# Columns of the first conditioning chunks: two plain transpositions and a reduction on VectorE in place of four selection products

## The chip, the core and the metric

One core of a Trainium2 chip runs the kernel as one program. The metric is the device time of that program in microseconds (us). The times given are of whole runs; a profile is of one execution, and its span (first to last instruction) is a little shorter than the run's own time.

## The reference

The reference is one step of a hybrid encoder layer for 640 tokens: 512 of one new stream and 16 of each of eight running streams. With c the conditioning vectors of the nine streams, it computes

```
sc  = silu(c)
mod = sc @ w_ada + b_ada                      # 9 x 1024 values a stream, split into shift, scale, gate
hn  = rmsnorm(x, norm_g) * (1 + scale1) + shift1
x   = x + 0.5 * gate1 * swiglu(hn, w1, w2)    # first feed-forward block
...
```

and then a mixer (a gated MLP beside a state-space scan), a second feed-forward block and a final modulated norm. The change lies in the first two parts of `mod`, shift1 and scale1 (2 x 1024 columns of w_ada), which the first feed-forward block needs before its first product.

## The kernel before

Activations lie transposed: features on the 128 partitions, the 640 tokens along the free axis, eight tiles of 128 features. The feed-forward products take float32 operands that are split into a high and a low part in fp32r, three products for each (`hn_hi`, `hn_lo` and the weights' `slot` pairs).

The first norm. Each of the eight token tiles of features (order `FIRST_TILE`) passes through four engines. VectorE multiplies the 512 prompt tokens by the inverse root (L2137, `hnf`), POOL does it for the 128 sample tokens (L745). Then the modulation: ScalarE scales and shifts the prompt part (L1596, in place in `hnf`), POOL the sample part (L762, L763). ScalarE copies the tile to `hn_hi` (L1602), VectorE subtracts to get `hn_lo` (L2143), and TensorE multiplies it with the weights of the first pair of hidden tiles (L1035, 12 products a tile). Between the tiles' work ScalarE and VectorE also split weight blocks (`slot`, L1546 and L2121).

The conditioning chunks. The 2 x 1024 columns come as eight chunks s of 256 columns (`ADA_FIRST`, order `FIRST_CHUNK`: a shift chunk, then the scale chunk of the same two feature tiles). A chunk takes these steps:

- `first_rows`, `cond_rows` (L985): TensorE multiplies the conditioning with the chunk. The contraction of 1024 is cut into eight pieces of 128, and piece k goes to the 32 partitions of row group k mod 4, so `ch_rows` in PSUM bank pair pC holds four partial sums, in row groups of 32 partitions of which nine are used.
- L1609: ScalarE copies the 128 x 256 partial sums to `ada_row` and raises `ch_row`.
- `first_cols`, `chunk_cols` (L993): for each of the chunk's two feature tiles TensorE multiplies the 128 x 128 block of `ada_row`, as stationary operand, with the selection matrix `quadsum` (128 x 9), which adds the four row groups and turns rows to columns in one go. `ch_tr` is raised. Before it TensorE waits for `ch_row` of this chunk, and for `ch_sum` of the chunk two before.
- `first_scale(q)` on VectorE (L2229, L2235), for the chunks 2q and 2q + 1: add the bias `b_col` to both, into `modc`, then (1 + scale) * norm_g in place, which raises `mod_ready`. ScalarE's L1596 and POOL's L762 wait for `mod_ready`.

The order of TensorE's work is written out by hand in `plain_first`: before the products of tile j it does the rows of the chunks in `FIRST_ROWS[j]` and the columns of those in `FIRST_COLS[j]`.

```
FIRST_ROWS = {0: (0, 1), 1: (2, 3), 2: (4,), 3: (5,), 4: (6, 7)}
FIRST_COLS = {0: (0, 1), 1: (2, 3), 3: (4, 5), 4: (6, 7)}
```

`keep_clock` issues products with no use (L1011), three behind the rows of chunk 0 and six before the products of tile 0. VectorE's order is that of `norm_first`: four L2137, `first_scale(0)`, two weight blocks, `hn_lo` of tile 0, two blocks, `hn_lo` of tile 1, four L2137, and then for each further pair of tiles `first_scale` and two `hn_lo`. ScalarE's order puts the copies L1609 of chunks 6 and 7 around `hn_hi` of tile 5.

Later chunks of the conditioning (`duo_rows`, `duo_cols`, `duo_sum`; L966, L977, L2221, L2222) use plain transpositions: L977 turns a 128 x 128 block with `nc.tensor.transpose`, and VectorE adds the parts.

Of the kernel before, what the change touches and what calls it, by code (L numbers as in the profile page):

```python
# [8 lines left out]
ALU = mybir.AluOpType  # L9
AX = mybir.AxisListType  # L10

P = 128
# [6 lines left out]
BANK = 512  # L19
# [3 lines left out]
NSTR = 1 + DEC_BATCH  # L23
# [13 lines left out]
QUAD = 32  # L37
# [47 lines left out]
def trunk_program(nc, x_prompt, x_sample, state_ssm, state_conv, c_prompt, c_sample, w_ada, b_ada, norm_g,  # L85
# [11 lines left out]
    def sem(name):  # L97
# [13 lines left out]
    modc = sb("modc", [P, MODT, NSTR])  # L111
    gate = sb("gate", [P, 3, KD * GRP])
    par = sb("par", [P, N_PAR])
    ident = sb("ident", [P, P])
# [15 lines left out]
    b_col = sb("b_col", [P, MODT])  # L130
    c_f32 = sb("c_f32", [P, KD, QUAD])
    quadsum = sb("quadsum", [P, QUAD])
# [89 lines left out]
    pB = ps("pB", 2 * BANK)  # L222
# [24 lines left out]
    ch_mm, ch_row, ch_tr, ch_sum = (  # L247
        sem("ch_mm"), sem("ch_row"), sem("ch_tr"), sem("ch_sum"))
# [100 lines left out]
    ch_rows = [pC[:, i * BANK:i * BANK + ADA_COLS] for i in range(2)]  # L349
    q_rows = [pB[:, q * ADA_COLS:(q + 1) * ADA_COLS] for q in range(2)]  # L350
    q_cols = [pB[:, BANK + q * 2 * P:BANK + (q + 1) * 2 * P] for q in range(2)]
    ch_cols = [pB[:, i * BANK:i * BANK + 2 * NSTR] for i in range(2)]


    xdt, xds = sq[:, 0:HG * HDIM], xadd[:, 0:HG * HDIM]
# [472 lines left out]
    def _(pe):  # L828
        mm = nc.tensor.matmul
# [101 lines left out]
        for k in range(KD):  # L931
            last = mm(pB[:, k * NSTR:(k + 1) * NSTR], c_sil[0:NSTR, k * P:(k + 1) * P], ident[0:NSTR, 0:NSTR],
                      start=True, stop=True)
        last.then_inc(c_tr, 1)

        for c in range(TT):
            pe.wait_ge(x_in[c], 16)
            wait(pe, xt_done, c - 1)
            for f in range(KD):
                last = nc.tensor.transpose(acc[c % 2][:, f * P:(f + 1) * P], x_row[c][:, f * P:(f + 1) * P],  # L940
                                           ident[:, :])
# [5 lines left out]
           start=True, stop=True).then_inc(par_tr, 1)  # L947
# [41 lines left out]
        def chunk_cols(i, m, bank, row):  # L989

            pe.wait_ge(ch_row, i + (m + 1))
            for f in range(2):
                last = mm(ch_cols[bank][:, f * NSTR:(f + 1) * NSTR], row[:, f * P:(f + 1) * P], quadsum[:, 0:NSTR],  # L993
                          start=True, stop=True)
            last.then_inc(ch_tr, 1)

        def first_rows(s):
# [250 lines left out]
        for c in range(TT):  # L1248
            last = mm(pC[:, c * QUAD:(c + 1) * QUAD], sq[0:2 * QUAD, c * P:(c + 1) * P], quadsum[0:2 * QUAD, :],
                      start=True, stop=True)  # L1250
# [13 lines left out]
        for j in range(CT):  # L1264
            dst = (acc[(U_Z + 1) % 2][0:TAIL, j * P:(j + 1) * P] if j < 8 else pC[0:TAIL, (j - 8) * P:(j - 7) * P])
            last = mm(dst, tails[:, j, :], ident[:, :], start=True, stop=True)
# [4 lines left out]
        for s in range(TT * SSD_G):  # L1271
            c, g = divmod(s, SSD_G)
            tok = slice(c * P, (c + 1) * P)
            dst = pB[:, s * P:(s + 1) * P] if c < ST else pC[:, BANK + g * P:BANK + (g + 1) * P]
            last = mm(dst, bcf[:, g, tok], bcf[:, SSD_G + g, tok], start=True, stop=True)
# [11 lines left out]
        for j in range(HP):  # L1287
            last = mm(pC[:, 3 * nh + j * DEC_BATCH:3 * nh + (j + 1) * DEC_BATCH],
                      gd[:, :, :].rearrange("p a b -> p (a b)")[:, j * P:(j + 1) * P], stream_of[:, :],
                      start=True, stop=True)  # L1290
# [110 lines left out]
        for j in range(HP):  # L1401
            last = nc.tensor.transpose(pC[:, j * P:(j + 1) * P], hst[:, j * P:(j + 1) * P], ident[:, :])
# [622 lines left out]
    def _(dve):  # L2025
        V = nc.vector
        st = Steps(dve, dve_step)
# [196 lines left out]
        def first_scale(q):  # L2224

            for s in (2 * q, 2 * q + 1):
                dve.wait_ge(ch_tr, s + 1)
                m = 2 * FIRST_CHUNK[s]
                V.tensor_tensor(out=modc[:, m:m + 2, :], in0=ch_cols[s % 2].rearrange("p (f c) -> p f c", c=NSTR),  # L2229
                                in1=b_col[:, m:m + 2].unsqueeze(2).broadcast_to([P, 2, NSTR]), op=ALU.add  # L2230
                                ).then_inc(ch_sum, 1)
            dve.wait_ge(ch_sum, 2 * q + 2)
            g = par[:, R_NORM + m - KD:R_NORM + m - KD + 2].unsqueeze(2).broadcast_to([P, 2, NSTR])
            v = modc[:, m:m + 2, :]
            V.scalar_tensor_tensor(out=v, in0=v, scalar=1.0, in1=g, op0=ALU.add, op1=ALU.mult).then_inc(mod_ready, 1)  # L2235
            dve.wait_ge(mod_ready, q + 1)
# [360 lines left out]
        s = ST * SSD_G  # L2597
# [205 lines left out]
```

## Time and profile before

| | |
|---|---|
| runs | 1444.98 us median of 3 (1444.59 to 1446.67) |
| the profiled execution, its own time | 1445.09 us |
| its span | 1443.5 us |
| TensorE (PE) busy | 1423.8 us, 99% of the span |
| VectorE (DVE) busy | 1014.8 us, 70% |
| ScalarE (ACT) busy | 662.8 us, 46% |
| POOL busy | 69.3 us, 5% |
| mean granted TensorE clock | 0.999 |

Busy time says how long an engine had instructions in it, not what it was worth. Matmuls overlap, so a row of the timeline that says 1.25 us for eight of them gives the time from the first's start to the last's end. A float32 product is issued as two instructions and is counted twice in the trace; a transposition with `nc.tensor.transpose` is counted once. PEld is the load of the stationary operand that goes before each of them.

### The profile page before, as it was taken

How to read it: one execution, taken by the hardware profiler on the slowest of the kernel's cores; microseconds unless marked ns; L12 is line 12 of the kernel's file. 1: busy time of each engine (PE TensorE's matmuls, PEld its weight loads, DVE VectorE, ACT ScalarE, POOL GpSimd, SP SyncE). 2: the span in 40 equal slices, each digit the busy share in tenths (PEclk: the TensorE clock that was granted, in tenths of full speed). 3: DMA queues.
4: the chain of work that ended last, by engine and by line, in shares of the span. 5: the costliest groups of instructions: out<-in, count | busy, mean ns of one | idle time of the engine just before them, and what ended most of it. 6: DMA issues, size and time to landing. Idle time of an engine off the chain costs nothing.

```text
span 1443.5 us, 25683 instructions
## 1 busy us (share of the span) xinstructions
PE 1423.8 (99%) x10212; PEld 1373.4 (95%) x10212; DVE 1014.8 (70%) x1742; ACT 662.8 (46%) x1186; POOL 69.3 (5%) x121
## 2 busy tenths in 40 slices
PE   7999999999999999999999999999999999999998
PEld 6899999999999999999789999998999999999997
DVE  5667667676777776667886567557767686767776
ACT  5543525253435444576825453226425253444354
POOL 3000000000000130000100000004000000000001
PEclk9999999999999999999999999999999999999999
DMA  9762434445344612231362222444314223231221
GB/s 304 208 196 66 153 116 143 121 133 160 110 139 132 183 31 74 74 93 55 98 187 77 68 73 64 131 144 122 110 56 144 66 89 88 69 107 52 81 74 74
DMA packets 219532, 161.02 MB, mean 112 GB/s; under 512 B 6826, under 2 KB 204646, under 8 KB 219426
## 3 DMA queue, kind: packets, MB, share of 16 engines
q1 hardware_dynamic: 217026, 153.87, 35.8%
q0 software_dynamic: 1696, 5.56, 1.3%
q8 instruction: 74, 1.21, 0.3%
q14 instruction: 32, 0.26, 0.1%
q10 hardware_dynamic: 704, 0.12, 0.0%
HBM read 151.50 MB, written 8.03 MB: 111 GB/s over the span
## 4 chain that ended last, share of the span: by engine, by line
PE 95%; DVE 2%; DMA 1%; ACT 1%; issue 0%; SPq 0%; POOL 0%; DVEq 0%; ACTq 0%
PE acc L844 25%; PE acc L1175 19%; PE pC L1066 19%; PE acc L1066 14%; PE acc L1054 4%; PE acc L1124 2%; PE pB L966 2%; PE acc L1035 1%; DMA ada_raw<-in_w_ada 1%; PE pC L1315 1%; PE pB L925 1%; PE pB L1300 1%; PE pC L1450 1%; PE pC L1334 1%; PE acc L861 0%; DVE y_row L2761 0%
## 5 line engine op out<-in xcount | busy, mean ns | idle before, releaser
L1546 ACT ACTIVATE slot<-raw 128x512 fp32r<-128x512 f32 (+1 forms) x310 | 189.5, 616 | 237.8 <-PE acc L1175 137.7
L2121 DVE TENSOR_TENSOR slot<-raw,slot 128x512 fp32r<-128x512 f32 (+1 forms) x310 | 208.1, 675 | 53.1 <-ACT slot L1546 50.6
L1175 PE MATMUL acc<-hid_hi,slot 128*128 128x320 f32 x1240 | 238.4, 310 | 0.0
L1066 PE MATMUL pC<-hn_hi,slot 128*128 128x320 f32 x912 | 216.3, 309 | 0.0
L1175 PEld LDWEIGHTS acc<-hid_hi,slot 128*128 128x128 f32 x1240 | 195.1, 188 | 2.9 <-issue 2.1
L844 PE MATMUL acc<-hn_hi,whi 128*128 128x320 f32 x672 | 160.9, 321 | 0.0
L1066 PEld LDWEIGHTS pC<-hn_hi,slot 128*128 128x128 f32 x912 | 156.2, 188 | 2.5 <-issue 2.5
L844 PE MATMUL acc<-hn_hi,wlo 128*128 128x320 f32 x672 | 153.1, 309 | 0.0
L844 PE MATMUL acc<-hn_lo,whi 128*128 128x320 f32 x672 | 152.9, 309 | 0.0
L1066 PE MATMUL acc<-tT,slot 128*128 128x320 f32 x912 | 146.3, 309 | 0.0
L1175 PE MATMUL acc<-hid_lo,slot 128*128 128x320 f32 x620 | 142.0, 308 | 0.0
L1066 PE MATMUL pC<-hn_lo,slot 128*128 128x320 f32 x456 | 140.8, 309 | 0.0
L1066 PEld LDWEIGHTS acc<-tT,slot 128*128 128x128 f32 x912 | 136.5, 188 | 0.0
L844 PEld LDWEIGHTS acc<-hn_hi,whi 128*128 128x128 f32 x672 | 111.9, 188 | 6.3 <-issue 5.9
L844 PEld LDWEIGHTS acc<-hn_lo,whi 128*128 128x128 f32 x672 | 112.3, 188 | 0.0
L844 PEld LDWEIGHTS acc<-hn_hi,wlo 128*128 128x128 f32 x672 | 112.2, 188 | 0.0
L1175 PEld LDWEIGHTS acc<-hid_lo,slot 128*128 128x128 f32 x620 | 103.8, 188 | 0.0
L2065 DVE TENSOR_TENSOR xadd<-acc,gate 128x128 f32<-128x128 f32 x95 | 27.6, 290 | 91.4 <-PE acc L1175 77.5
L2035 DVE TENSOR_TENSOR wlo<-wraw,whi 128x1024 fp32r<-128x1024 f32 x50 | 61.0, 1222 | 38.2 <-ACT whi L1528 37.6
L1066 PEld LDWEIGHTS pC<-hn_lo,slot 128*128 128x128 f32 x456 | 85.6, 188 | 0.0
L2059 DVE SCALAR_TENSOR_TENSOR xT<-acc,gate,xT 128x320 f32<-128x320 f32 (+1 forms) x190 | 82.6, 475 | 0.2 <-PE acc L861 0.2
L1066 PE MATMUL pC<-tT,slot 128*128 128x320 f32 x456 | 73.2, 309 | 0.0
(389 smaller groups left out, 2414.9 us busy)
## 6 DMA issues: line engine op xcount, KB each, us to landing
raw<-in_ffn_w SPq DMA_DIRECT2D x88, 512.0 KB, 5.2
sraw<-in_w_ada SPq DMA_DIRECT2D x26, 1024.0 KB, 6.5
wraw<-in_w_in SPq DMA_DIRECT2D x36, 512.0 KB, 3.8
raw<-in_ffn_w SPq DMA_DIRECT2D x16, 1024.0 KB, 5.1
ada_raw<-in_w_ada SPq DMA_DIRECT2D x8, 1024.0 KB, 11.7
wraw<-in_w_out SPq DMA_DIRECT2D x16, 512.0 KB, 4.1
raw<-in_ffn_w SPq DMA_DIRECT2D x8, 768.0 KB, 4.4
sraw<-in_w_ada_final SPq DMA_DIRECT2D x6, 1024.0 KB, 7.5
```

What stands on the lines that cost most here:

```text
L844: last = mm(acc[p][:, h * BANK:h * BANK + HALF], w[:, k, :], a[:, k * TOK + h * HALF:k * TOK + (h + 1) * HALF], start=(k == 0 and t == 0), ...
L925: last = nc.tensor.transpose(out[:, c * P:(c + 1) * P], src[:, c * P:(c + 1) * P], ident[:, :])
L966: last = mm(q_rows[lane_of(duo)][q * QUAD:(q + 1) * QUAD, :], c_f32[:, k, :], kxn(duo_raw(duo, j), KD, ADA_COLS)[:, k, :], start=(kk == 0) ...
L1054: last = mm(half(acc[d], h), w[:, kk * P:(kk + 1) * P], a[:, k * TOK + h * HALF:k * TOK + (h + 1) * HALF], start=(k == 0 and t == 0), stop ...
L1066: last = mm(out, w[:, kk * P:(kk + 1) * P], a, start=(first and kk == 0 and t == 0), stop=(kk == KQ - 1 and t == 2), skip_group_check=not ...
L1124: last = mm(a[h], w[t // 2][:, k, :], (hid_hi, hid_lo)[t % 2][:, k * TOK + h * HALF:k * TOK + (h + 1) * HALF], start=(k == 0 and t == 0), ...
L1175: last = mm(a[h], w[t // 2][:, k, :], (hid_hi, hid_lo)[t % 2][:, k * TOK + h * HALF:k * TOK + (h + 1) * HALF], start=(k == 0 and t == 0), ...
L1546: A(slot_as(fi, b, 0), source_of(fi, b), ACT.Copy).then_inc(blk_hi, 1)
L2035: V.tensor_tensor(out=weights(n, i, 1, w), in0=wraw[p][:, 0:w], in1=weights(n, i, 0, w).bitcast(F32), op=ALU.subtract).then_inc(wlo_done, 1)
L2059: return V.scalar_tensor_tensor(out=x[:, s:e], in0=a[s // HALF][:, p:p + e - s], scalar=gate[:, q, f * GRP:f * GRP + 1], in1=x[:, s:e], op ...
L2065: V.tensor_tensor(out=by_stream(xadd[:, SEQ:TOK]), in0=by_stream(a[1][:, SEQ - HALF:HALF]), in1=g, op=ALU.mult)
L2121: V.tensor_tensor(out=slot_as(fi, b, 1), in0=source_of(fi, b), in1=slot_as(fi, b, 0).bitcast(F32), op=ALU.subtract).then_inc(blk_lo, 1)
```

## The change

For the first eight chunks the two selection products become two plain transpositions with the identity. A transposition only turns the block, so the four row groups come out as four groups of 32 columns, and `ch_cols` is 256 columns wide instead of 18. VectorE then adds the four groups with a `tensor_reduce` (nine columns used of each), and adds the bias in an instruction of its own, in place in `modc`. `ch_sum`, for which TensorE waits before it writes the bank again, now follows the reduction. VectorE waits for its own reduction before the bias, and for the bias before it goes on.

```diff
-    ch_cols = [pB[:, i * BANK:i * BANK + 2 * NSTR] for i in range(2)]
+    ch_cols = [pB[:, i * BANK:i * BANK + 2 * P] for i in range(2)]
...
             pe.wait_ge(ch_row, i + (m + 1))
             for f in range(2):
-                last = mm(ch_cols[bank][:, f * NSTR:(f + 1) * NSTR], row[:, f * P:(f + 1) * P], quadsum[:, 0:NSTR],
-                          start=True, stop=True)
+                last = nc.tensor.transpose(ch_cols[bank][:, f * P:(f + 1) * P], row[:, f * P:(f + 1) * P], ident[:, :])
             last.then_inc(ch_tr, 1)
...
             for s in (2 * q, 2 * q + 1):
                 dve.wait_ge(ch_tr, s + 1)
                 m = 2 * FIRST_CHUNK[s]
-                V.tensor_tensor(out=modc[:, m:m + 2, :], in0=ch_cols[s % 2].rearrange("p (f c) -> p f c", c=NSTR),
-                                in1=b_col[:, m:m + 2].unsqueeze(2).broadcast_to([P, 2, NSTR]), op=ALU.add
-                                ).then_inc(ch_sum, 1)
-            dve.wait_ge(ch_sum, 2 * q + 2)
+                part = ch_cols[s % 2].rearrange("p (f k c) -> p f c k", f=2, c=QUAD)[:, :, 0:NSTR, :]
+                V.tensor_reduce(out=modc[:, m:m + 2, :], in_=part, axis=AX.X, op=ALU.add).then_inc(ch_sum, 1)
+                dve.wait_ge(ch_sum, s + 1)
+                st.done(V.tensor_tensor(out=modc[:, m:m + 2, :], in0=modc[:, m:m + 2, :],
+                                        in1=b_col[:, m:m + 2].unsqueeze(2).broadcast_to([P, 2, NSTR]), op=ALU.add))
```

On TensorE, at the columns of chunks 0 and 1 (one row stands for the four instructions of a pair of chunks; each pair has the same):

```order
-L993 MATMUL pB<-quadsum,ada_row 128x9 x4
-L1011 MATMUL acc<-upto,ident 128x256 x6
-L1035 MATMUL acc<-hn_hi,slot 128x320 x2
...
+L993 MATMUL pB<-ident,ada_row 128x128 x4
+L1010 MATMUL acc<-upto,ident 128x256 x6
+L1034 MATMUL acc<-hn_hi,slot 128x320 x2
```

Nothing changes its place; four products with nine columns to stream become four transpositions with 128, and all line numbers behind fall by one.

On VectorE, at `first_scale(1)`, between the products with the inverse root and the low parts of tiles 2 and 3:

```order
-L2137 TENSOR_TENSOR hnf<-xT,rT 128x512 x4
-L2229 TENSOR_TENSOR modc<-pB,b_col 128x18 x2
...
+L2136 TENSOR_TENSOR hnf<-xT,rT 128x512 x4
+L2229 TENSOR_REDUCE modc<-pB 128x18
+L2231 TENSOR_TENSOR modc<-modc,b_col 128x18
+L2229 TENSOR_REDUCE modc<-pB 128x18
+L2231 TENSOR_TENSOR modc<-modc,b_col 128x18
 L2235 SCALAR_TENSOR_TENSOR modc<-modc,par 128x18
```

Two instructions ahead of the scale became four, each behind the one before it. The same is so in all four calls.

## Rows read from the trace of the kernel before

**Rows 1.** The profile's page, busy time of TensorE, share of the span, instructions
```profile
PE 1423.8 (99%) x10212; PEld 1373.4 (95%) x10212; DVE 1014.8 (70%) x1742; ACT 662.8 (46%) x1186; POOL 69.3 (5%) x121
```

**Rows 2.** Waits of TensorE, whole span: us in total, times, longest
```profile
PE acc L1035 <- DVE hn_lo L2143: 2.6, 3, 1.8
...
PE acc L1054 <- ACT tmp L1706: 0.4, 1, 0.4
```

**Rows 3.** Chain that ended last, from 20 us: start, us, what
```profile
22.85 0.41 DVE modc L2235
...
23.35 0.81 ACT hnf L1596
...
27.07 2.02 PE acc L1035 x12
...
32.38 0.19 DVE modc L2235
...
35.34 2.02 PE acc L1035 x12
...
44.72 0.19 DVE modc L2235
...
51.26 0.60 ACT tmp L1706
...
51.99 14.32 PE acc L1054 x96
```

**Rows 4.** Timeline, TensorE's column products and weight loads of chunks 6 and 7
```profile
43.19 1.28 PE L993 MATMUL pB<-quadsum,ada_row 128*128 128x9 f32 x8
...
43.86 0.52 PEld L993 LDWEIGHTS pB<-quadsum,ada_row 128*128 128x128 f32 x4 [0.15 <-issue]
```

**Rows 5.** Timeline, ScalarE's copies of chunks 3 and 7, and `hn_hi` between
```profile
31.02 0.38 ACT L1609 ACTIVATE ada_row<-pC 128x256 f32<-128x256 f32 x1 [0.48 <-PE pC L985]
...
43.37 0.38 ACT L1609 ACTIVATE ada_row<-pC 128x256 f32<-128x256 f32 x1
```

**Rows 6.** Timeline, the transpositions of a later chunk, loads and products
```profile
82.14 0.29 PEld L977 LDWEIGHTS pB<-ident,srow 128*128 128x128 f32 x2
82.29 0.38 PE L977 MATMUL pB<-ident,srow 128*128 128x128 f32 x2
```

**Rows 7.** Timeline of VectorE, `first_scale` of pairs 1 and 3
```profile
31.54 0.18 DVE L2229 TENSOR_TENSOR modc<-pB,b_col 128x18 f32<-128x18 f32 x1
32.17 0.18 DVE L2229 TENSOR_TENSOR modc<-pB,b_col 128x18 f32<-128x18 f32 x1 [0.46 <-PE pB L993]
32.38 0.18 DVE L2235 SCALAR_TENSOR_TENSOR modc<-modc,par 128x18 f32<-128x18 f32 x1
...
43.51 0.82 DVE L2143 TENSOR_TENSOR hn_lo<-hnf,hn_hi 128x640 fp32r<-128x640 f32 x1 [0.82 <-ACT hn_hi L1602]
44.25 0.44 DVE L2229 TENSOR_TENSOR modc<-pB,b_col 128x18 f32<-128x18 f32 x2
```

**Rows 8.** VectorE's reductions and small additions, ns min/median/max or mean
```profile
L2221 DVE TENSOR_TENSOR modc<-pB,b_col x18: 184/188/191, 83.2 to 1133.0; 128x36 f32<-128x36 f32 x18
...
L2202 DVE TENSOR_REDUCE quadsum<-ident x1: 371/371/371, 6.0 to 6.0; 128x32 f32<-128x128 f32 x1
...
L2664 DVE TENSOR_REDUCE stat<-pB 128x5 f32<-128x640 f32 x8 | 6.6, 827 | 2.0 <-PE pB L925 2.0
```

**Rows 9.** Timeline of POOL, its eight products for the sample tokens
```profile
17.72 5.51 POOL L745 TENSOR_TENSOR hnf<-xT,rT 128x128 f32<-128x128 f32 x8 [11.14 <-ACT rT L1556]
```

**Rows 10.** Stretches: length, busy time and instructions of each engine, granted clock (PEclk)
```profile
10.00:15.00 5.00, 4.65 (x30) 4.17 (x29) 4.35 (x4) 4.89 (x10) 0.00 (x0) 1.00 0.78 242
24.00:27.00 3.00, 1.29 (x6) 0.79 (x5) 2.21 (x4) 3.00 (x7) 1.05 (x3) 1.00 1.01 324
1436.00:1438.00 2.00, 0.35 (x4) 0.11 (x1) 2.00 (x4) 0.00 (x0) 0.00 (x0) 1.00 1.03 381
1438.00:1440.00 2.00, 0.00 (x0) 0.00 (x0) 2.00 (x4) 0.00 (x0) 0.00 (x0) 0.82 1.03 382
```

## The prediction

> **What bounds the kernel now.** Read the busy times first: TensorE had instructions in it for 99% of the span [rows 1]. Then its waits, because only where it waits can something else set the end: over the whole span it waits for `hn_lo` three times, 2.6 us in all, and once 0.4 us for ScalarE's `tmp` [rows 2]. Everything that the change touches lies between 18 and 50 us. So the question is when TensorE can begin the product row L1054, at 51.99 in the chain [rows 3]. From there the chain is almost nothing but TensorE until the last norm, so a shift of that moment should reach the end in full.
>
> What does 51.99 hang on? Follow the chain back. TensorE waits there for ScalarE's `tmp`, which starts at 51.26, and ScalarE is fed without a break by what `first_scale(3)` released: VectorE's last scale at 44.72 [rows 3]. Between the two lie the modulation of tiles 6 and 7, a table load, three weight blocks and the silu, all in ScalarE's own order: 51.99 - 44.72 = 7.27 us of fixed work. The first product of tile 0 (27.07) and that of tile 2 (35.34) hang in the same way on the scales at 22.85 and 32.38 [rows 3]. The eight chunks are thus a latency chain (rows on TensorE, copy on ScalarE, columns on TensorE, `first_scale` on VectorE), four times over, each beginning where the last one let TensorE or ScalarE go on. I price the change by how much later each of the four scales starts.
>
> **TensorE's side.** Before, a chunk's columns are four records, a pair of chunks eight; now a chunk has two. If TensorE were the bound this would count in full, but the second chunk of a pair has to wait for its copy. Chunk 7's copy runs 43.37 to 43.75 [rows 5], and its first weight load starts at 43.86 [rows 4], 0.11 later. Chunk 3's copy ends at 31.40 [rows 5] and VectorE is released by that chunk's columns at 32.17 [rows 7]. So the second chunk's columns begin when ScalarE is ready, before and after. What the first chunk's columns save turns into a wait for the copy, and I cost it at nothing; its cover is that copy, and were the copy earlier by 0.3 us, the saving would show. What counts is the second chunk's own length, from first load to result. Before, the products' row ends at 43.19 + 1.28 = 44.47, that is 0.61 us behind the load at 43.86 [rows 4]. A pair of transpositions runs from 82.14 to 82.29 + 0.38 = 82.67, so 0.53 us [rows 6]. That is a gain of 0.08; I take 0.1, as VectorE's start needs its few hundredths either way. The bounds are 0 and 0.2.
>
> **VectorE's side.** Before, an addition is followed by the scale 0.21 us later (32.17 to 32.38 [rows 7]). Now the same path is reduction, bias, scale. The bias reads 18 elements and should cost the 0.21 once more. The reduction reads 72 elements of PSUM and is not in the trace in this shape. Its bounds are 0.18 us (an addition of 18 elements [rows 7]) and 0.37 (the reduction of 128 elements, the engine's first instruction [rows 8]). Between them, an addition of 36 elements takes 0.188 and the reduction of 640 elements 0.827 [rows 8], a slope of 0.64 / 604 = 1.06 ns an element, which gives 0.188 + 36 x 1.06 ns = 0.23 us. I take 0.23, as 72 is much nearer to 36 than to 640, and 0.26 from its start to the next one's. So a chunk takes 0.26 + 0.21 = 0.47 us of VectorE, where it took 0.21.
>
> **The four pairs.** The delay of each scale against the one before it:
> - Pair 0. The columns give 0.1 back, the second chunk's path grows by 0.26: +0.16. POOL is still in its eight products until 17.72 + 5.51 = 23.23 [rows 9], and the scale at 22.85 took 0.41 where the later ones take 0.19 [rows 3]. The added bias instructions meet the same company, up to +0.22 each; or the scale itself, coming later, is rid of it, -0.22. I take +0.2, with ends of 0 and +0.5.
> - Pair 1. VectorE comes to it at 31.54 [rows 7], when the first chunk is ready; reduction and bias take it to 32.01, before the second chunk's 32.07. So +0.26 - 0.1 = +0.16.
> - Pair 2. VectorE waits there for both chunks. +0.16 again.
> - Pair 3. Here VectorE is late itself: `hn_lo` of tile 5 starts at 43.51 and the two additions come right behind it, at 44.25 and at 44.51, where the second was just released [rows 7]. Before, the scale began 44.72 - 44.25 = 0.47 us behind the first addition. Now two reductions and two biases stand there, 2 x 0.47 = 0.94 us. So +0.47, and the columns' gain is worth nothing, since chunk 7 is ready (44.4) before VectorE has done with chunk 6 (44.7).
>
> The sum is 0.2 + 0.16 + 0.16 + 0.47 = 0.99, so **+1.0 us**. On TensorE it first appears as a longer wait ahead of tile 0 (1.8 us, the longest one [rows 2]) and ahead of tile 2, then as a new wait of some 0.4 us ahead of tile 6, whose `hn_lo` hangs on pair 3; and then L1054 begins 1.0 us later. Nothing is moved in any queue, no DMA is added, and the loads wait for the chunks' rows, not for their columns. The span becomes 1443.5 + 1.0 and the profiled execution 1445.09 + 1.0 = 1446.1. That execution lies 0.1 above the median of the three runs, 1444.98, so the median becomes **1446.0 us**. About 0.2% (2.9 us) is what a measurement of this kernel can tell from no change; the runs themselves span 2.1 us. The forecast is well inside it.
>
> The Trainium skill speaks against this sum: "Perfetto Trace Analysis", section "Transposes", says to use a transpose and not a standard matmul for what is logically a transposition, since it skips the arithmetic. By it the sum would be a gain, that of the first rival. No sentence above rests on it.
>
> **The rivals.**
> - *TensorE paces it, and the columns' saving counts.* Before, the eight records of a pair occupy 1.28 us [rows 4]. Two transpositions occupy 0.38 [rows 6], so four take at most 0.76. That saves 0.52 a pair and 2.1 us over four: 1442.9 us, or, where it counts only in a pair or two, up to 1444.6. For it speaks that TensorE is busy 99% [rows 1]; against it the copy that ends only 0.11 ahead of the load [rows 4, 5]. Chance 0.12. Even whole it stays within 0.2%.
> - *The reduction is slow.* Groups of four elements, 32 apart, in PSUM may cost as the 0.37 row does [rows 8]. Then +0.14 in pairs 0 to 2 and +0.28 in pair 3, 0.7 more, and with pair 0 at its upper end 1.0 more: 1446.7 to 1447.0 us. Chance 0.15.
> - *The clock falls.* This one is slower than before for certain. Transpositions might not count as work, and TensorE is idle longest right behind them, 1.8 us ahead of tile 0 [rows 2]. With pair 0 that becomes 2.0. At the end of the program TensorE is idle from about 1436.4, and the granted clock is 1.00 until 1438 and 0.82 over the next two microseconds [rows 10], so it fell at 1438 + 2 x 0.64 = 1439.3, some 2.9 us into the idle time. From about that length on this rival decides; 2.0 is short of it, and the half-busy stretch 24 to 27 was at 1.00 [rows 10]. Were it to fall to its lower level of 1.2 GHz at 27.07, the work until the columns of pair 1 (27.07 to 31.5) would take twice as long, +4.4: with the forecast's 1.0, 1450.4 us. Chance 0.05.
> - *The shift is swallowed.* A later wait of TensorE with another cause than the shifted engines could take it in. Against it speaks that the chain goes on from 51.99 with TensorE without a break, 14.32 us in its first row alone [rows 3]. Time 1445.0. Chance 0.08.
>
> On the clock, row and rule part. TensorE did little but transpositions between 10 and 15 us, 30 instructions in 4.65 us, at a granted 1.00 [rows 10]; so the transpositions that are added do not lower it by themselves. The Trainium skill, "TensorE: Matmul & The Clock Gate", section "Part 4: PE-mode transpose", says that the full clock doesn't engage for transposes, as they don't count as busy in the same way. By the rule the time would be the clock rival's 1450.4, by the row the forecast's.
>
> **How the numbers follow.** Forecast 0.60, the four rivals 0.12, 0.15, 0.05 and 0.08. The forecast's own range is 1445.4 to 1446.6 by the bounds of pair 0 and of the columns. For 8 in 10 it has to reach to the slow reduction, 1447.0, and take in the swallowed shift and the smaller part of TensorE's saving, 1444.6; with a few tenths on either side for the median of a few runs, **1444.3 to 1447.3**. Faster by over 0.2% means below 1442.1, beyond even the whole of TensorE's saving: 0.02. Slower by over 0.2% means above 1447.9: the clock rival and a small rest, 0.06. Within: 0.92.
>
> **What the next profile shows.** The second chunk's transpositions start about 0.1 us behind ScalarE's copy, with TensorE waiting for it in each pair, and end 0.5 us later. Reductions of 0.23 us and bias additions of 0.18. The first, second and fourth scale start at about 23.0, 32.7 and 45.7; tile 0's products at 27.3, tile 2's at 35.7, L1054 at 53.0. The granted clock stays 1.00 until the last microseconds. I am wrong if L1054 starts no later than 51.99 (TensorE paced the stretch), if the reduction takes over 0.35, or if L1054 is late by 1.0 and the end is not.

## The result and the profile after

| | kernel before | changed kernel |
|---|---|---|
| median of 20 executions each | 1445.54 us | 1448.20 us |
| lowest, highest | 1444.59, 1449.39 | 1446.44, 1450.74 |
| ratio | | 1.0018, 95% interval 1.0012 to 1.0025 |
| profiled execution, own time and span | 1445.09, 1443.5 us | 1450.30, 1448.7 us |
| TensorE busy | 1423.8 us | 1425.0 us |
| VectorE busy | 1014.8 us | 1017.0 us |
| mean granted clock, this execution | 0.999 | 0.996 |

The changed kernel is slower by 2.7 us by the medians and 2.6 by the means, where 1.0 was forecast, and its time lies above the range of 1444.3 to 1447.3. The median of 1448.20 is 2.2 above the forecast's 1446.0, and 0.56 of that is the kernel before itself, whose median over 20 executions is 1445.54 and not the 1444.98 of the first three. Counted from that kernel the range ended at +2.3, and 2.7 is above that too. The ratio is below the 0.2% that was called no change, while its interval reaches beyond 0.2% and leaves out a ratio of 1.

Start where the prediction said the answer would stand, with the chain, which answers to [rows 3]. The rows give start, length and what ran.

```profile
23.01 0.19 DVE modc L2235
...
27.00 2.47 PE acc L1034 x12
29.47 3.06 PE pC L985 x32
...
34.08 0.19 DVE modc L2235
...
37.03 2.02 PE acc L1034 x12
...
41.65 0.19 DVE modc L2235
...
46.95 0.19 DVE modc L2235
...
54.22 5.81 PE acc L1053 x38
```

L1054 of before is L1053 now, and it starts at 54.22 instead of 51.99. Two rows give the first clue. Tile 0's products take 2.47 us from start to the next piece, those of tile 2 2.02 as before; and the rows of chunks 2 and 3 take 3.06 us, where the chain of before has 1.86 for the same 32 records:

```profile
29.09 1.86 PE pC L985 x32
```

Nothing in the change touches these. The stretches (length, then busy time and instructions of PE, PEld, DVE, ACT and POOL, then the granted clock, the DMA's share and GB/s) say why:

```profile
24.00:26.00 2.00, 0.74 (x4) 0.31 (x2) 1.28 (x2) 2.00 (x5) 0.98 (x3) 1.00 1.05 343
26.00:28.00 2.00, 1.00 (x7) 1.00 (x8) 2.00 (x4) 1.97 (x4) 0.00 (x0) 1.00 1.07 344
28.00:30.00 2.00, 2.00 (x15) 1.44 (x18) 1.83 (x4) 0.28 (x1) 0.00 (x0) 0.59 1.09 356
30.00:32.00 2.00, 2.00 (x28) 0.94 (x24) 1.55 (x3) 0.38 (x1) 0.00 (x0) 0.56 1.09 347
32.00:34.00 2.00, 1.76 (x21) 1.15 (x10) 0.78 (x4) 0.38 (x1) 0.00 (x0) 1.00 1.09 348
...
622.00:624.00 2.00, 2.00 (x9) 1.75 (x8) 1.68 (x3) 1.16 (x3) 0.00 (x0) 0.57 0.60 144
```

In the kernel before, the same stretches stand at 1.00:

```profile
28.00:30.00 2.00, 2.00 (x28) 1.46 (x30) 1.83 (x4) 0.35 (x1) 0.00 (x0) 1.00 1.10 351
30.00:32.00 2.00, 1.95 (x29) 1.30 (x21) 1.72 (x4) 0.77 (x2) 0.00 (x0) 1.00 1.09 348
```

In the changed kernel the granted clock fell to its lower level of 1.2 GHz at about 28.4 and came back shortly before 32. It did not fall while TensorE idled but 1.4 us after it had taken up tile 0. It fell a second time near 622 us. The timeline of TensorE shows what stood ahead of the first fall:

```profile
21.13 1.01 PE L993 MATMUL pB<-ident,ada_row 128*128 128x128 f32 x4
21.98 2.76 PE L1010 MATMUL acc<-upto,ident 128*128 128x256 f32 x12
27.00 0.56 PE L1034 MATMUL acc<-hn_hi,slot 128*128 128x320 f32 x2 [2.26 <-DVE hn_lo L2142]
```

In the kernel before the same three pieces were

```profile
21.42 1.19 PE L993 MATMUL pB<-quadsum,ada_row 128*128 128x9 f32 x8
22.46 2.84 PE L1011 MATMUL acc<-upto,ident 128*128 128x256 f32 x12
27.07 0.56 PE L1035 MATMUL acc<-hn_hi,slot 128*128 128x320 f32 x2 [1.77 <-DVE hn_lo L2143]
```

The wait ahead of tile 0 is 2.26 us; it was 1.77. Two things lengthen it: VectorE gives `hn_lo` later, and TensorE is through with the unused products earlier, because the transpositions ahead of them are short.

VectorE's new instructions, ns min/median/max, are as priced but for one bias addition of 0.455 us, and answer to [rows 8]:

```profile
L2229 DVE TENSOR_REDUCE modc<-pB x8: 225/232/233, 21.6 to 46.5; 128x18 f32<-128x72 f32 x8
...
L2231 DVE TENSOR_TENSOR modc<-modc,b_col x8: 177/178/455, 21.9 to 46.7; 128x18 f32<-128x18 f32 x8
```

The distances along the latency chain, in us, tell latency and clock apart. Each is the difference of two starts; "rows 1" is the start of the rows of chunk 1, scales are L2235, "products" is L1054 or L1053. The last columns belong to experiments below.

| from, to | before | change | predicted addition | e1, nine unused products | e4, one group |
|---|---|---|---|---|---|
| rows 1, tile 0 | 6.65 | 6.87 | 0.20 | 6.66 | 6.26 |
| tile 0, scale 1 | 5.31 | 7.08 | 0.16 | 5.52 | 5.28 |
| scale 1, scale 2 | 7.41 | 7.57 | 0.16 | 7.57 | 7.24 |
| scale 2, scale 3 | 4.93 | 5.30 | 0.47 | 5.31 | 4.88 |
| scale 3, products | 7.27 | 7.27 | 0 | 7.27 | 7.28 |
| sum | 31.57 | 34.09 | 0.99 | 32.33 | 30.94 |

From tile 0 to scale 1 the fall of the clock sits: with it 7.08, without it 5.47 to 5.52 (e1, e13, and e10, a second profile of the change). So the clock cost 1.6 us there, and the latency is 0.22 + 0.16 + 0.16 + 0.37 = 0.9 us in this execution. The 0.22 of pair 0 is its least certain part. The other three profiles of the change (e10, e14, e15) have 6.59, 6.59 and 6.60 us from rows 1 to tile 0, and the five profiles with the columns and VectorE's part of before have 6.43 to 6.65. The first scale starts 0.17 later (2.60 us behind rows 1 against 2.43), but in the profile of before it took 0.40 us itself, and in these three 0.18. The whole distance from rows 1 to products is 32.20 to 32.33 us in e1, e10 and e13, which have no fall near 28, and 31.57 before: 0.6 to 0.8 us of latency. The profiled execution started this stretch 0.29 earlier, hence 2.23 at L1053 and not 2.52. From there to the end 3.0 us more are lost, none of them in the change's reach: 0.9 by 107 us, where a load of `raw` came late and TensorE waited 0.7 us behind it, 1.5 in the fall near 622, and 0.6 around a load of `gm_bias`, for which TensorE waited 0.7. These differ from one execution to the next, as the experiments show, so one pair of profiles can't be subtracted.

### The profile page after: what moved, and what is told of

It reads as the page before. It is cut to its first block, busy times and chain, and to the rows that moved or that the text cites. A ratio compares the mean times of both kernels' runs of the same rounds, so it can differ in the third digit from the quotient of the medians.

```text
span 1448.7 us, 25663 instructions
## 1 busy us (share of the span) xinstructions
PE 1425.0 (98%) x10196; PEld 1372.4 (95%) x10196; DVE 1017.0 (70%) x1750; ACT 662.3 (46%) x1186; POOL 69.3 (5%) x121
## 4 chain that ended last, share of the span: by engine, by line
PE 92%; DVE 3%; DMA 2%; ACT 1%; SPq 1%; issue 1%; POOL 0%; DVEq 0%; ACTq 0%
PE acc L844 24%; PE acc L1174 19%; PE pC L1065 18%; PE acc L1065 13%; PE acc L1053 4%; PE pB L966 2%; PE acc L1123 2%; PE acc L1034 1%; PE pC L1314 1%; DMA ada_raw<-in_w_ada 1%; DMA raw<-in_ffn_w 1%; PE pB L925 1%; PE pB L1299 1%; PE pC L1449 1%; PE pC L1333 1%
```

## The experiments

The theory after the result: **latency**, 0.6 to 0.9 us, where 0.99 was predicted, and **the clock**, which falls in more executions because TensorE has more idle time ahead of tile 0. The rival: the clock's falls are chance, or come from the transpositions themselves. A timed run has eleven executions, beside 15 or 33 of the kernel before on the same chip. The mean granted clock of an execution is known for each of them, and it follows the number of falls, if roughly: of the 17 profiles, those without a fall before the last microseconds have 0.998 or 0.999, those with one 0.997 or 0.998, those with two 0.996. Of 96 executions of the kernel before, the clock was 0.999 in 38 (mean time 1445.4 us), 0.998 in 43 (1446.6), 0.997 in 14 (1446.9) and once 0.995 (1449.8), on average 0.9982. Of the change's 20 only one was at 0.999 (1446.4), six at 0.998, seven at 0.997 and six at 0.996 (mean 1450.1), on average 0.9971. The difference of 0.0011 is about that of one fall more in an execution.

| run | edit | ratio to before | interval | mean clock | mean time |
|---|---|---|---|---|---|
| change | | 1.0018 | 1.0012 to 1.0025 | 0.9971 | 1448.5 |
| e1 | change, nine unused products | 1.0008 | 0.9999 to 1.0017 | 0.9984 | 1446.9 |
| e13 | change, seven | 1.0010 | 1.0001 to 1.0019 | 0.9980 | 1447.9 |
| e9 | e1, one bias a pair | 1.0001 | 0.9992 to 1.0010 | 0.9983 | 1446.5 |
| e3 | before, VectorE's part of the change | 1.0014 | 1.0005 to 1.0023 | 0.9975 | 1447.9 |
| e4 | change, VectorE's part of before | 1.0005 | 0.9996 to 1.0014 | 0.9976 | 1446.8 |
| e8 | e4, nine unused products | 0.9994 | 0.9985 to 1.0003 | 0.9987 | 1445.1 |
| e2 | before, five unused products | 0.9999 | 0.9990 to 1.0008 | 0.9981 | 1445.8 |
| e6 | before, three | 1.0012 | 1.0003 to 1.0021 | 0.9965 | 1447.9 |
| e5 | before, nine | 1.0003 | 0.9994 to 1.0012 | 0.9983 | 1446.3 |
| e7 | before, 25 transpositions for the six | 0.9997 | 0.9988 to 1.0006 | 0.9985 | 1445.5 |

### e1: the change, with nine unused products ahead of tile 0

```diff
-                    keep_clock(6)
+                    keep_clock(9)
```

> The change with nine instead of six unused products ahead of tile 0. They took 2.76 us for six in the profile of the change, so nine end about 1.4 us later, at 26.1, still ahead of tile 0 at 27.0, and TensorE's idle time there falls from 2.3 to 0.9 us. Theory of the clock: the fall at 28.4 is gone, the scale of pair 1 follows tile 0 by 5.4 us (7.1 with the fall), L1053 begins at about 52.6, and the time is 1.0 to 1.5 us above the kernel before, not 2.7. Theory of latency alone: the clock fell by chance and unused products change nothing, 2.7 us above. If the products get in tile 0's way, its first product comes later than 27.0.

The timeline of TensorE in this run:

```profile
21.50 4.05 PE L1010 MATMUL acc<-upto,ident 128*128 128x256 f32 x18
26.31 0.56 PE L1034 MATMUL acc<-hn_hi,slot 128*128 128x320 f32 x2 [0.76 <-DVE hn_lo L2142]
```

And the stretches, with the granted clock third from the end:

```profile
26.00:28.00 2.00, 1.69 (x11) 1.69 (x12) 1.84 (x4) 1.55 (x3) 0.00 (x0) 1.00 1.09 347
28.00:30.00 2.00, 2.00 (x35) 0.98 (x33) 2.00 (x4) 0.39 (x1) 0.00 (x0) 1.00 1.09 349
```

The idle time ahead of tile 0 is 0.76 us, the clock holds at 1.00, and the mean over the executions is back at 0.9984, that of the kernel before. The distances of the table show the latency alone, 32.33 - 31.57 = 0.76 us. The mean time is 1.6 us below the change's, for three more products without use, which the theory of latency alone can't give. The two intervals of the table overlap, but the difference itself is clear: by the scatter of the 20 and the 11 executions it is 1.6, give or take 0.9.

### e2: the kernel before, with five unused products

```diff
-                    keep_clock(6)
+                    keep_clock(5)
```

> The kernel before with five instead of six unused products, so that TensorE's idle time ahead of tile 0 grows from 1.8 to 2.2 us, as in the changed kernel, and nothing else is changed. Theory of the clock: in a part of the executions the clock falls near 28 us, each fall costs some 1.6 us, and the median rises by 0.5 to 1.6 us; the mean granted clock shows it (0.998 or less, 0.999 without). Theory of latency alone: within 0.2 us of the kernel before.

The wait ahead of tile 0 was 2.08 us in its profile. Time and clock (0.9981) are those of before. The theory of the clock, in the plain form that 2.1 us of idle time is enough, is not borne out by this run.

### e3: the kernel before, with VectorE's part of the change

```diff
-                V.tensor_tensor(out=modc[:, m:m + 2, :], in0=ch_cols[s % 2].rearrange("p (f c) -> p f c", c=NSTR),
-                                in1=b_col[:, m:m + 2].unsqueeze(2).broadcast_to([P, 2, NSTR]), op=ALU.add
-                                ).then_inc(ch_sum, 1)
-            dve.wait_ge(ch_sum, 2 * q + 2)
+                V.tensor_copy(modc[:, m:m + 2, :], ch_cols[s % 2].rearrange("p (f c) -> p f c", c=NSTR)).then_inc(ch_sum, 1)
+                dve.wait_ge(ch_sum, s + 1)
+                st.done(V.tensor_tensor(out=modc[:, m:m + 2, :], in0=modc[:, m:m + 2, :],
+                                        in1=b_col[:, m:m + 2].unsqueeze(2).broadcast_to([P, 2, NSTR]), op=ALU.add))
```

> The kernel before with its selection products, but VectorE's part as in the change: a copy out of PSUM, then the bias as an instruction of its own, each waited for. Theory of latency: pairs 1 and 2 are 0.21 us longer, pair 3 by 0.4, pair 0 by 0.2, and L1054 begins 1.0 us later. Idle time ahead of tile 0 is 2.0 us. If the clock holds at 2.0, the time is 1.0 us above; if 2.0 is already too long in some executions, up to 2.0 above.

The four distances to scale 3 are 6.96, 5.85, 7.68 and 5.19 us, together 25.68 against 24.30. Of these 1.38 us 0.3 aren't VectorE's: the rows of chunks 2 and 3 took 2.21 us instead of 1.93 in this execution. The other 1.05 are, in sum, what was expected, though spread otherwise (pair 3 has 0.26, expected were 0.4). Here is pair 1:

```profile
32.24 0.18 DVE L2231 TENSOR_TENSOR modc<-modc,b_col 128x18 f32<-128x18 f32 x1
32.72 0.18 DVE L2229 COPY modc<-pB 128x18 f32<-128x18 f32 x1 [0.30 <-PE pB L993]
32.93 0.18 DVE L2231 TENSOR_TENSOR modc<-modc,b_col 128x18 f32<-128x18 f32 x1
33.15 0.18 DVE L2235 SCALAR_TENSOR_TENSOR modc<-modc,par 128x18 f32<-128x18 f32 x1
```

Copy, bias and scale start 0.21 apart, as priced. VectorE's part alone makes the kernel slower, 1.0014, clear of no change, and the clock is 0.9975, against 0.9983 for the kernel before beside it, at the same wait of 2.08 us ahead of tile 0 that did nothing in e2. The one profile of e3 has no fall near 28, so where its additional falls lie isn't shown.

### e4, e11, e12: the transpositions with VectorE's part of before

The sum over the row groups 1 to 3 is left out; the bias is added to group 0 as read from PSUM.

```diff
-                V.tensor_reduce(out=modc[:, m:m + 2, :], in_=part, axis=AX.X, op=ALU.add).then_inc(ch_sum, 1)
-                dve.wait_ge(ch_sum, s + 1)
-                st.done(V.tensor_tensor(out=modc[:, m:m + 2, :], in0=modc[:, m:m + 2, :],
-                                        in1=b_col[:, m:m + 2].unsqueeze(2).broadcast_to([P, 2, NSTR]), op=ALU.add))
+                V.tensor_tensor(out=modc[:, m:m + 2, :], in0=part[:, :, :, 0],
+                                in1=b_col[:, m:m + 2].unsqueeze(2).broadcast_to([P, 2, NSTR]), op=ALU.add
+                                ).then_inc(ch_sum, 1)
+            dve.wait_ge(ch_sum, 2 * q + 2)
```

> The transpositions of the change with VectorE's part of before: one addition of the bias to the first row group alone. It leaves out the sum over the other three row groups. Theory of latency: every scale about 0.1 us earlier than before, so 0.3 us below the kernel before. TensorE's saving does not come through as such (2 us would if it paced). Theory of the clock: the unused products end 0.3 us earlier, idle time ahead of tile 0 is 2.0 us, and if the clock falls there in part of the executions the gain is lost, 0 to 1 above.

> Transpositions with VectorE's part of before (the sum over three row groups left out), once more. Its eleven executions had a mean granted clock of 0.9976, its first profile a fall near 620 us alone. If a second place exists ahead of or in tile 0's products, this profile may show it; a fall between 32 and 50 us would mean that the waits for the copies lower the clock by themselves.

> As the look before, a third profile of the same kernel: a fall near 28 us, near 620 us, in both places, or in neither. Where none is near 28 us, tile 0 to scale 1 takes 5.3 us again.

The chain is 0.6 us shorter than before (30.94 against 31.57), twice what I expected, 0.4 of it ahead of tile 0. Not all of it is the transpositions': 0.22 of the 0.4 is the first scale, which takes 0.18 us here and 0.40 in the profile of before, but also 0.18 in e5 and e6, which have the columns of before. The first scale starts 0.17 earlier, and pair 2 gives the same 0.17. In e11 the chain is 30.55, 1.0 shorter. So the transpositions give 0.4 to 0.8 us; far from the 2.1 us of a kernel that TensorE paces. But the kernel is no faster: the mean clock is 0.9976. The three profiles show one fall each: near 620 (e4), near 18 (e11), and near 28 us (e12). The third one, with a wait of 1.95 us ahead of tile 0:

```profile
26.00:28.00 2.00, 0.98 (x4) 0.98 (x5) 2.00 (x4) 1.97 (x4) 0.00 (x0) 0.83 1.09 352
28.00:30.00 2.00, 2.00 (x9) 1.95 (x8) 2.00 (x4) 0.14 (x1) 0.00 (x0) 0.50 1.09 349
30.00:32.00 2.00, 2.00 (x30) 0.94 (x32) 1.40 (x3) 0.37 (x1) 0.00 (x0) 0.81 1.09 348
```

### e8: the same with nine unused products

The edit is that of e1 on top of that of e4.

> The transpositions with VectorE's part of before (the sum over three of the four row groups left out), and nine unused products. With six it was 0.6 us above before on average at a lower mean granted clock, 0.9976 against 0.9983. If those additional falls lie ahead of or in tile 0's products, nine products remove them: clock 0.9983 or more, and 0.3 to 0.6 us below before. If they lie elsewhere, it stays at 0.6 above.

Mean clock 0.9987, the highest of all, eight of eleven executions at 0.999, and a mean 1.7 us below e4 by three unused products alone (1.6 when each is counted from the kernel before beside it, as the two ran on different chips). So e4's additional falls hang on TensorE's work ahead of tile 0, and without them the transpositions' gain comes out: 1445.1 us on average, 0.9994, an interval that just holds no change. In the one profile of e8 a load of `raw` came late and the wait ahead of tile 0 was 1.59 us even so, without a fall.

### e5, e6: the kernel before, with nine and with three unused products

> The kernel before with nine unused products instead of six; idle time ahead of tile 0 some 0.4 us instead of 1.8. In 33 executions of the kernel before the mean granted clock was 0.999 in 12, 0.998 in 18 and 0.997 in 3. If part of those falls lie near 28 us, they go, and the time is up to 0.5 us below before. If all lie elsewhere (near 620 us in three profiles), nothing changes: within 0.2 us.

> The kernel before with three unused products instead of six: idle time ahead of tile 0 about 3.1 us. Theory that idle time ahead of tile 0 makes the clock fall: a fall near 28 us in nearly every execution, the profile shows it, mean granted clock 0.0012 lower than before's, and 1.6 us or more above. Theory that idle time has no part in it: clock and time as before.

With three, the wait ahead of tile 0 is 3.0 us. The products of tile 0 follow at half pace, by the timeline of TensorE:

```profile
22.30 1.54 PE L1011 MATMUL acc<-upto,ident 128*128 128x256 f32 x6
26.85 0.90 PE L1035 MATMUL acc<-hn_hi,slot 128*128 128x320 f32 x2 [3.01 <-DVE hn_lo L2143]
```

And the stretches, with the granted clock third from the end:

```profile
26.00:28.00 2.00, 1.15 (x4) 1.15 (x5) 2.00 (x4) 1.94 (x3) 0.00 (x0) 0.62 1.09 348
28.00:30.00 2.00, 2.00 (x10) 1.98 (x8) 2.00 (x5) 0.00 (x0) 0.00 (x0) 0.53 1.09 348
```

Not one of eleven executions was at 0.999, the mean clock is 0.0017 lower and the time 1.0012. Tile 0 to scale 1 took 6.68 us, 1.4 more than before. So less work of TensorE ahead of tile 0 does make the clock fall, with nothing else changed. With nine there is no gain (1.0003, clock 0.9983), which fits a kernel before with hardly any falls there. The profile of e5 has the one near 620 us:

```profile
620.00:622.00 2.00, 2.00 (x9) 1.91 (x9) 1.97 (x3) 1.65 (x4) 0.00 (x0) 0.50 0.84 250
```

That fall thus comes without the change too. It cost e5 and e1 some 1.5 us between the late conditioning rows near 504 and near 987 us (484.1 us apart in both, and 482.6 in the profile of before).

### e7: unused transpositions in place of unused products

```diff
-                    keep_clock(6)
+                    keep_turning(25)
...
+            for i in range(n):
+                nc.tensor.transpose(acc[1][:, (i % 2) * P:(i % 2 + 1) * P], upto[:, 0, :], ident[:, :])
```

> The kernel before with its six unused products replaced by 25 unused transpositions of the same total length (25 at 0.11 = 2.75 us, against 2.8). Theory that transpositions don't count as work for the clock: it falls near 28 us in nearly every execution, 1.6 us or more above before, mean granted clock 0.0012 lower. Theory that they count: clock and time as before, within 0.3 us.

The timeline of TensorE, with the transpositions in L1016:

```profile
21.96 2.93 PE L1016 MATMUL acc<-ident,upto 128*128 128x128 f32 x25
26.52 0.56 PE L1040 MATMUL acc<-hn_hi,slot 128*128 128x320 f32 x2 [1.64 <-DVE hn_lo L2148]
```

And the stretches, with the granted clock third from the end:

```profile
26.00:28.00 2.00, 1.48 (x10) 1.48 (x11) 2.00 (x4) 1.61 (x3) 0.00 (x0) 1.00 1.09 347
28.00:30.00 2.00, 2.00 (x32) 1.19 (x34) 2.00 (x4) 0.38 (x1) 0.00 (x0) 1.00 1.09 349
```

Clock 0.9985 and time 0.9997: transpositions hold the clock as well as products. With three unused products, e6, it was 0.9965. The rival that they don't count as work is out.

### e9: one bias addition a pair

```diff
-                dve.wait_ge(ch_sum, s + 1)
-                st.done(V.tensor_tensor(out=modc[:, m:m + 2, :], in0=modc[:, m:m + 2, :],
-                                        in1=b_col[:, m:m + 2].unsqueeze(2).broadcast_to([P, 2, NSTR]), op=ALU.add))
+            dve.wait_ge(ch_sum, 2 * q + 2)
+            both = modc[:, m - KD:m + KD, :].rearrange("p (a t) c -> p a t c", a=2)[:, :, 0:2, :]
+            bias = b_col[:, m - KD:m + KD].rearrange("p (a t) -> p a t", a=2)[:, :, 0:2]
+            st.done(V.tensor_tensor(out=both, in0=both, in1=bias.unsqueeze(3).broadcast_to([P, 2, 2, NSTR]), op=ALU.add))
```

> The change with nine unused products, and one bias addition for both chunks of a pair instead of two: VectorE does reduction, reduction, bias, scale. Theory of latency: pairs 0 to 2 as in the change with nine products, since the first bias hides there behind the wait for the second chunk; in pair 3, where VectorE is late, one addition of 0.21 us goes, so the distance from scale 2 to scale 3 falls from 5.31 to 5.10 us. In time 0.2 us below the change with nine products, 0.5 us above the kernel before. If it is more than 0.2 on the path, the first bias was not hidden in the other pairs.

The timeline of VectorE at pair 3:

```profile
44.66 0.36 DVE L2229 TENSOR_REDUCE modc<-pB 128x18 f32<-128x72 f32 x2
45.06 0.20 DVE L2233 TENSOR_TENSOR modc<-modc,b_col 128x36 f32<-128x36 f32 x1
45.29 0.18 DVE L2236 SCALAR_TENSOR_TENSOR modc<-modc,par 128x18 f32<-128x18 f32 x1
```

Scale 2 to scale 3 is 4.98 us, 0.33 less than in e1 and not 0.21: the two reductions, with no wait between them, take 0.36 us together instead of 2 x 0.26. In time it is even with the kernel before, 1.0001. It has the lowest mean of the forms of the change that compute everything, 0.4 us below e1, which eleven executions don't tell from nothing, and it does not beat the kernel before.

### e13, e14, e15, e10: seven unused products, and further profiles of the change

> The change with seven unused products instead of six, so that TensorE's idle time ahead of tile 0 is 1.8 us as before the change. If the length of the idle time alone brings the additional falls: mean granted clock 0.9983 as in the kernel before, and 0.9 us above it. If it is the transpositions or the other waits of the change: mean clock 0.9971 to 0.9975 and 2 to 2.6 us above. In between, if the clock reacts to the whole work of the stretch and not to the idle time.

> The changed kernel once more, for a second profile. By the mean granted clocks (0.9971 against 0.9984 with nine unused products) nearly every execution has a fall between the idle time ahead of tile 0 and pair 1. The profile should show it between 26 and 32 us, with an idle time of 2.0 to 2.3 us before it; without it, pair 1's scale follows tile 0 by 5.4 to 5.5 us.

> The changed kernel, a third profile: a fall near 28 us by the theory of the idle time, unless one ended shortly before (near 18 us, as in the second). A fall near 622 us is as likely as in the kernel before.

> The changed kernel, a fourth profile, with the same expectation: a fall near 28 us, or one near 18.

With seven the mean clock is 0.9980 and the mean time 1447.9, between the change with six and with nine: most of the clock is back with about 0.4 us more work. The ratio, 1.0010, is nearer to e1's 1.0008 than to the change's 1.0018, but eleven executions don't part it clearly from either. The four profiles of the change have falls near 28 us (the first and e14), near 18 us (e10), and in e15 none in this stretch, behind a wait of 2.00 us ahead of tile 0, but a wait of 0.67 us for the weights of chunk 3. The profile of e13 has a fall near 18 us too, and none near 28. All four profiles of the change have one near 620. In e14 the wait ahead of tile 0 was 1.99 us, tile 0 to scale 1 took 6.99. In e10, where the clock had come back at about 21.2, the same wait of 1.99 us brought no fall, and tile 0 to scale 1 was 5.49:

```profile
18.00:20.00 2.00, 2.00 (x17) 0.94 (x10) 2.00 (x3) 0.29 (x1) 1.76 (x4) 0.50 1.19 297
20.00:22.00 2.00, 2.00 (x10) 1.37 (x13) 1.33 (x2) 0.09 (x1) 1.84 (x3) 0.69 0.90 234
26.00:28.00 2.00, 0.48 (x3) 0.07 (x1) 1.82 (x3) 2.00 (x5) 0.44 (x2) 1.00 1.05 354
```

The falls near 18 us can't be the change's doing. They begin at about 18, in e10, e11 and e13 alike, and in all three the first changed instruction, the columns of chunk 0, starts at 22.9 or later. The unused products whose number e1, e8 and e13 change stand behind it too. So what these experiments give back on the clock are falls that lie later.

## Why the prediction was wrong

**What held.** The chain that it read was the right one: L1053 follows scale 3 by 7.26 to 7.28 us in every profile (L1054 in the kernels with the columns of before, L1059 in e7). The second chunk's transpositions wait for ScalarE's copy. The reduction took 0.232 us (predicted 0.23), the bias 0.178. Pairs 0 to 2 cost 0.22, 0.16 (without the clock's part) and 0.16 us, as priced. In part this is luck. The 0.22 of pair 0 is one execution's, and other profiles have next to nothing there. The 0.16 of pair 1 is made of two misses that cancel: the second chunk's columns took 0.42 us instead of 0.60, a gain of 0.18 and not 0.1, and VectorE took the result up 0.09 us behind them instead of 0.02. Pair 3 cost 0.37 and not 0.47. The error there is in the start: VectorE takes up the pair 0.11 us earlier, counted from scale 2 (46.00 - 41.65 against 44.25 - 39.79); from there to the scale it is 0.95 us, predicted 0.94. In all 0.9 us of latency in the first profile and 0.6 to 0.8 in the others without a fall near 28, against 0.99. Executions whose clock was 0.999 agree: 1446.4 us for the change (one), 1446.2 for e1 (six), against 1445.4 for the kernel before (38).

**What failed** is the term that the sum put at nothing, the clock: "The granted clock stays 1.00 until the last microseconds", with a fall as a rival at 0.05. Of that rival one sentence was incomplete and two were wrong.
- "With pair 0 that becomes 2.0." Three of the four profiles of the change do have 1.99 or 2.00 us, but on another ground than pair 0. I had costed what the first chunk's columns save on TensorE at nothing, because the copy hides it. On the path it is hidden. But the unused products stand right behind the columns, and they moved forward with them, by 0.27 us measured from the rows of chunk 1 (4.61 against 4.88 us to their end). With the 0.22 of pair 0 that made 2.26 us in the first profile, without it the 2.0 of the others.
- "It fell some 2.9 us into the idle time", taken from the end of the program as the point from which the rival decides. The end of the program shows a fall after TensorE had been idle for long; it doesn't show that a shorter gap in a half-busy stretch is safe. Here the clock fell 1.4 us after the gap of 2.26 had ended, in e12 behind a gap of 1.95, in e14 behind 1.99. The stretch from 24 to 27, less than half busy at 1.00, was one execution, and I took it for all.
- The price, +4.4, assumed that the lower clock lasts to the columns of pair 1 and doubles all work until then. It cost 1.6 in the first profile, and 1.5 in e14.

So it was no rival of 1 in 20 with a large price, but an addition to the forecast itself: by the mean clock about one fall more in an execution, at some 1.5 us. The sum with the measured parts: 0.6 to 0.9 of latency, and 0.0011 of mean clock (0.9982 - 0.9971) x 1447 us = 1.6, together 2.2 to 2.5. Measured are 2.6 by the means and 2.7 by the medians of the 20. That nine unused products take away 1.6 us (1448.5 to 1446.9) and 0.0013 of clock, with no other edit, shows this part.

The Trainium skill's page "TensorE: Matmul & The Clock Gate", section "Part 4: PE-mode transpose", warned of the clock for another reason, that transpositions don't engage the full clock. e7 disagrees: 25 of them in place of six products, clock 0.9985. Its warning pointed to the right rival by the wrong mechanism. "Perfetto Trace Analysis", section "Transposes", prefers them to products; e4's chain agrees with 0.6 us of the 31.6, and the reduction and the second addition take it back.

The rival that TensorE paces is refuted by that same chain, 0.6 us shorter in e4 and 1.0 in e11 against 2.1. The slow reduction is refuted by its 0.232 us. A ratio beyond 0.2% was given a small chance and didn't come, if by little, but the range's upper end, 1447.3, took in no fall of the clock at all. Three runs of the kernel before spanned 2.1 us, and that spread was itself a hint: between executions at 0.999 and at 0.998 there are 1.2 us, which I had put down to noise.

**What stays open.** How many of the change's additional falls lie near 28 us: two of its four profiles have one, and four are too few. All four also have the fall near 620 us, which 5 of the 13 other profiles have; the mean clock of e1 (0.9984) speaks against a cause in the change, but two profiles more or less would say otherwise. And the length of the wait alone doesn't decide: 2.08 us did nothing in e2 (0.9981) and went with more falls in e3 (0.9975), e15 had 2.00 and e4 1.65 without a fall. In e10, e11 and e13 a fall near 18 us stands and none near 28, behind waits of 1.99, 1.65 and 1.55 us; whether the one keeps the other away isn't shown. With eleven executions a run I can't say more.

## What to carry to other kernels

An engine's saving that the critical path hides is not free of effect: it moves the work behind it in the queue, and where that work is there to bridge a gap, the gap grows. Before a latency chain on TensorE is changed, list its idle gaps with the work on both sides, and test a version with a few more or fewer unused products: that costs two runs and separates clock from latency. Where a change trades one instruction on TensorE for two in a row on VectorE inside such a chain, count starts: 0.21 us for each dependent small instruction, times the number of links.

## What was not expected of the hardware

- A fall of the clock near 620 us stands in 9 of the 17 profiles, of kernels with and without the change. It begins where TensorE's rows are busy without a gap: in e5 2.00 of 2.00 us in the stretches 616 to 618 and 618 to 620. It costs about 1.5 us between the rows near 504 and near 987 us (e1 and e5).
- The clock falls after a gap as well as in it: 0.2 (e14), 0.3 (e12) and 1.4 us (the first profile) after work was taken up again, and in e6 some 0.4 us before the wait of 3.01 us ended. Each of the four cost 1.4 to 1.6 us of the way from tile 0 to scale 1.
- Unused transpositions keep the clock up as well as products do (e7).
- Two `tensor_reduce` instructions of 72 elements without a wait between them start some 0.13 us apart instead of 0.26: 0.36 us for both (e9).
